# Gates gathered one step sooner, the last expert's table in the eighth step, expert results added as whole rows

## The chip, the cores and the metric

The kernel runs on one core of one Trainium2 chip. The metric is the device time of one execution in microseconds (us). A core has five engines with a queue each: TensorE (PE in the profile, its weight loads PEld), VectorE (DVE), ScalarE (ACT), GpSimd (POOL) and SyncE (SP), and 16 DMA engines that move data between the chip's memory (DRAM) and the core's own.

## The reference

One layer of a decoder on 512 new tokens and 64 tokens of running sequences, all in float32, width 1024. A mixer (a linear recurrence and a retention with running states) comes first. The part that matters here is the mixture of experts behind it: 16 experts in 4 groups, each token takes the best group and two experts in it.

```python
gates = jnp.sum(jax.nn.one_hot(expert_id, N_EXPERTS, dtype=F32)
                * (p_g[:, None] * top_w)[..., None], axis=1)
h = jax.nn.silu(jnp.einsum('nd,edf->nef', xf, w_g)) * jnp.einsum('nd,edf->nef', xf, w_u)
out = jnp.einsum('nef,efd->nd', h * gates[..., None], w_d)
```

Each expert has three matrices of 1 MB: `w_g` and `w_u` (1024 x 256) and `w_d` (256 x 1024). The result is normed, scaled and added to the tokens; the new retention states are outputs too.

## The kernel before

The first 350 us are the mixer and the routing; the change does not touch them. Then comes the loop over `NST` = 14 steps, numbered 0 to 13. Steps 0 to 2 hold experts 0 to 2, the others hold the remaining experts in the order of their token counts. Steps 5 and 9 (`paired(e)`) hold two small experts of up to 64 tokens each, all others one expert with up to 128. An expert's tokens are its up to 128 *slots*.

A step in the order in which it is worked on:

- `hits(e)` (VectorE, three steps ahead, `AHEAD` = 3) builds a 0/1 table of tokens by slots; `slot_tokens(e)` (TensorE, five small transposes or products) turns it into token numbers; `numbers(e)` (VectorE) writes them as indices.
- `gather_input(e)` (GpSimd, four indirect DMAs) fetches the tokens' rows to `xg`; `take_input(e)` (VectorE, one 128x1024 transpose, line 2443; for step 0 TensorE transposes and VectorE and ScalarE copy a half each, line 2435) turns them.
- `expert_in(e)` (TensorE) forms the gate and the up product, 32 instructions each; `pair_in(e)` does the same for a pair, in other PSUM banks. ScalarE takes silu of the first (semaphore `s_hs`), VectorE multiplies by the second (`s_hm`; line 2538, for a pair line 2534). A pair's product is transposed by `pair_turn`, in the middle of the next step's `expert_in`.
- `expert_out(e)`, `pair_out(e)` (TensorE) form the output, a pair's one step later. `take_out(e)` copies it times the gate to `eo[e % 2]`, ScalarE the first 512 columns (`s_eoa`), VectorE the last 512 (`s_eod`; lines 2453, 2457).
- The gates lie in `gates_dram`. `gather_gates(e)` (GpSimd, line 771) fetches the slots' rows of 16 gates to `gsl[e % 2]`; from step 3 on `pick_gates(e)` (VectorE, lines 2498 to 2502) picks the expert's column, and only then can `take_out(e)` run.
- `add_rows(e)` (GpSimd, line 782) adds `eo` to the tokens' rows in DRAM, with an indirect DMA that accumulates. There are two tables of 512 columns, `f_dram[0]` and `f_dram[1]`, and a chain of DMAs for each: each add waits (`s_ost`) until the add before it in its chain has landed, and `take_out(e)` waits until the add of step e - 2 has.

The last expert (step 13) is not added in DRAM: VectorE builds a table of tokens by slots times gate (`wlast`, lines 2543 to 2557, now in step 2), TensorE transposes it in steps 11 and 12 (`turn_last`) and multiplies it by the last results (`add_last`), while SyncE loads the sums from `f_dram` to `Y` (line 606). The closing chain on VectorE (`finish`) norms and adds.

All orders are written out by hand, one per engine. GpSimd's, in iteration j: `gather_input(j)`, `gather_gates(j - 2)`, `add_rows(j - 3)`. VectorE's, in step e: `hits(e + 3)`, the products, `take_input(e + 1)`, `numbers(e + 3)`, the pick, `take_out`. For step 9, a pair, `take_input(10)` comes ahead of the products. An engine works its list strictly in order. Before the loop VectorE has `numbers(2)`, `take_input(0)`, then `new_state` (heads 2 and 3 of the retention states, read from PSUM banks 4, 5, 1 and 6, line 2179; semaphore `s_snew`), then the gates (lines 2290 to 2521, `s_gw`). `expert_in(0)` waits for `s_snew` ahead of its up products, which write banks 1 and 6. The weights stream through 13 buffers of 1 MB, each loaded by SyncE as soon as TensorE is done with what it held.

Lines 811 and 814 are the helpers through which TensorE's products and transposes are recorded, line 1494 ScalarE's.

Of the kernel before, what the change touches and what calls it, by code (L numbers as in the profile page):

```python
# [16 lines left out]
P = 128  # L17
# [10 lines left out]
NH = 4  # L28
# [29 lines left out]
MORE = 4  # L58

# [122 lines left out]
def build(nc, x_prompt, x_sample, state_conv, state_lru, state_ret, c_prompt, c_sample, w_mod, b_mod,  # L182
# [6 lines left out]
    with ExitStack() as ctx:  # L189
# [3 lines left out]
        def sem(name):  # L193
# [8 lines left out]
        f_dram = [nc.dram_tensor(f"f_dram{c}", (6 * P, HALF), F32, kind="Internal").ap()  # L202
                  for c in range(2)]
# [97 lines left out]
        gsl = [region(14784 + i * NE, NE) for i in range(2)]  # L301
# [113 lines left out]
        s_ost = [[sem(f"s_ost{c}{i}") for i in range(2)] for c in range(2)]  # L415
# [79 lines left out]
        gpick = [tiny(144 + i, 1) for i in range(2)]  # L495
        lastr, lastg = tiny(152, TILES), tiny(160, TILES)
# [29 lines left out]
        def _(sp):  # L526
# [68 lines left out]
            with sp.Else():  # L595
# [4 lines left out]
                for t in END_ORDER:  # L600
                    for c in range(2):
                        if t == END_ORDER[0]:
                            sp.wait_ge(s_ost[c][0], 16 * (NST // 2))
                            sp.wait_ge(s_ost[c][1], 16 * ((NST - 1) // 2))
                        if t < TILES - 1:
                            sp.dma_start(Y[:, t, c * HALF:(c + 1) * HALF],
                                         f_dram[c][t * P:(t + 1) * P, :]).then_inc(s_fl[t], 16)
                        else:
                            sp.dma_start(Y[c * NS:(c + 1) * NS, t, 0:HALF], f_dram[c][SEQ:NTOK, :])\
# [19 lines left out]
        def _(pool):  # L629
# [54 lines left out]
            for c in range(2):  # L684
                pool.dma_start(f_dram[c].rearrange("(a p) d -> p a d", p=P),
                               consts[:, None, C_ZERO:C_ZERO + HALF].to_broadcast([P, 6, HALF]))\
                    .then_inc(s_fready, 16)
# [74 lines left out]
            with pool.Else():  # L762
                def gather_gates(e):
# [12 lines left out]
                def add_rows(e):  # L776
                    pool.wait_ge(s_add, e + 1)
                    for c in range(2):
                        pool.wait_ge((s_eoa, s_eod)[c], e + 1)
                        if e:  # L780
                            pool.wait_ge(s_ost[c][(e - 1) % 2], 16 * ((e - 1) // 2 + 1))
                        pool.indirect_dma_start(  # L782
                            out=f_dram[c], in_=eo[e % 2][:, c * HALF:(c + 1) * HALF],
                            in_offset=None, compute_op=ALU.add,
                            out_offset=bass.IndirectOffsetOnAxis(ap=add_tok[:, e:e + 1], axis=0),
                            bounds_check=NTOK - 1, oob_is_err=False)\
# [1829 lines left out]
```

## Time and profile before

| | before |
|---|---|
| median of 3 runs | 549.45 us (547.32 to 549.88) |
| the profiled execution | 548.57 us |
| its span | 546.6 us |
| mean granted clock of TensorE | 0.99 |
| TensorE busy | 522.1 us, 96% |
| VectorE busy | 259.3 us, 47% |
| GpSimd busy | 155.2 us, 28% |

The span is the time from the first to the last instruction in the trace; the rest of the profiled execution's time lies around it. All times in the trace count from the span's start. A line of a timeline gives start, length, engine, source line, operation, tiles (out<-in), shapes and how many instructions are merged in it; a bracket at its end is the idle time of the engine just before it and what ended that. The granted clock is 1.00 at 2.4 GHz and 0.50 at 1.2 GHz. "DMA to landing" is the time from an issue to the arrival of its last byte.

### The profile page before, as it was taken

What the parts mean: (1) busy time and instruction counts of PE and PEld (TensorE: products, weight loads), DVE (VectorE), ACT (ScalarE), POOL (GpSimd) and SP (SyncE); (2) the same over time, 40 slices, a digit from 0 to 9 for tenths busy, and PEclk for the clock granted to TensorE, in tenths of its full rate; (3) what the DMA queues carried; (4) which work ended last, traced back from release to release, by engine and by line L of the source; (5) the groups of instructions that cost most, each with busy time, mean ns of one, the idle gap of its engine ahead of it and who ended that gap; (6) DMA issues with size and microseconds to landing.
All of it is one profiled execution on the core that took longest, in us unless ns stands there. A gap on an engine that the chain in (4) does not pass through costs nothing.

```text
span 546.6 us, 7575 instructions
## 1 busy us (share of the span) xinstructions
PE 522.1 (96%) x2798; PEld 324.0 (59%) x2798; DVE 259.3 (47%) x759; ACT 151.3 (28%) x293; POOL 155.2 (28%) x166
## 2 busy tenths in 40 slices
PE   8999999999999999999999999788999899899994
PEld 6677755544455454557444445477787777577851
DVE  3443465443033143244453365684776545643347
ACT  7332497711123122132232333400010010000132
POOL 3017000116000000000210020347777747756500
PEclk8999999999999999999999999999999999999998
DMA  9999997899800000009820034879997999996474
GB/s 267 356 328 354 348 321 312 305 387 361 291 0 1 0 0 1 1 4 383 327 78 38 38 116 172 311 278 387 362 362 259 351 396 367 366 377 221 56 196 177
DMA packets 47417, 126.50 MB, mean 231 GB/s; under 512 B 6654, under 2 KB 19358, under 8 KB 41234
## 3 DMA queue, kind: packets, MB, share of 16 engines
q1 hardware_dynamic: 30912, 99.36, 49.6%
q0 software_dynamic: 11408, 22.05, 15.0%
q10 hardware_dynamic: 5058, 4.58, 2.5%
q8 instruction: 24, 0.39, 0.3%
q14 instruction: 15, 0.12, 0.1%
HBM read 116.48 MB, written 17.30 MB: 245 GB/s over the span
## 4 chain that ended last, share of the span: by engine, by line
PE 73%; DMA 10%; DVE 8%; issue 5%; POOL 3%; SPq 1%; ACT 0%; POOLq 0%; ACTq 0%; DVEq 0%
PE psum L811 71%; DMA arena<-gates_dram,slot_tok 5%; DMA ring<-in_w_mod_dram 3%; POOL arena L753 2%; PE psum L814 2%; DMA u_dram<-arena 2%; DVE arena L2378 1%; DVE x L2383 1%; DVE arena L2443 1%; DVE arena L2325 1%; DVE arena L2179 0%; SPq L574 0%; DVE arena L2457 0%; DVE arena L2319 0%; ACT arena L1494 0%
## 5 line engine op out<-in xcount | busy, mean ns | idle before, releaser
L811 PE MATMUL psum<-ring,uT 128*128 128x512 f32 (+1 forms) x384 | 126.5, 522 | 0.0
L811 PEld LDWEIGHTS psum<-ring,uT 128*128 128x128 f32 (+1 forms) x384 | 56.5, 172 | 60.1 <-issue 55.8
L1494 ACT ACTIVATE arena<-psum 128x512 f32<-128x512 f32 (+6 forms) x80 | 35.7, 476 | 164.7 <-PE psum L811 154.0
L811 PE MATMUL psum<-uT,ring 128*128 128x288 f32 x256 | 64.9, 410 | 0.1
L811 PEld LDWEIGHTS psum<-arena,ring 128*128 128x128 f32 x512 | 60.1, 196 | 6.8 <-issue 6.8
L811 PE MATMUL psum<-arena,ring 128*128 128x128 f32 x512 | 60.6, 280 | 3.7 <-DVE arena L2534 2.1
L753 POOL DMA_INDIRECT arena<-u_dram,part_tok x52 | 53.4, 1028 | 21.6 <-issue 14.3
L811 PEld LDWEIGHTS psum<-uT,ring 128*128 128x128 f32 x256 | 47.7, 190 | 16.4 <-issue 4.0
L811 PE MATMUL psum<-ring,arena 128*64 128x256 f32 (+2 forms) x192 | 50.6, 490 | 0.1
L782 POOL DMA_INDIRECT f_dram<-arena,add_tok x26 | 41.6, 1600 | 27.7 <-issue 13.1
L811 PE MATMUL psum<-arena 128*128 128x128 f32 (+6 forms) x253 | 42.3, 330 | 5.4 <-DVE arena L2325 2.4
L1494 ACT ACT_TABLE_LOAD x33 | 42.3, 1283 | 3.1 <-issue 2.1
L811 PEld LDWEIGHTS psum<-arena 128*128 128x128 f32 (+4 forms) x253 | 26.3, 157 | 21.0 <-issue 16.4
L811 PEld LDWEIGHTS psum<-ring,arena 128*64 128x64 f32 (+1 forms) x192 | 22.4, 154 | 22.8 <-issue 18.4
L699 POOL DMA_DIRECT2D out_dram<-arena x1 | 0.8, 829 | 123.8 <-DVE arena L2117 123.8
L811 PE MATMUL psum<-ring,hy 128*128 128x512 f32 (+1 forms) x80 | 32.9, 600 | 0.5 <-ACT arena L1494 0.5
L811 PE MATMUL psum<-ring,outbT 128*128 128x512 f32 (+1 forms) x80 | 32.4, 593 | 0.0
L1494 ACT ACTIVATE arena<-psum,uT 128x512 f32<-128x512 f32 x10 | 6.9, 688 | 77.2 <-DVE uT L2502 54.2
L2443 DVE STREAM_TRANSPOSE arena<-arena 128x1024 f32<-128x1024 f32 x13 | 26.4, 2028 | 0.0
L1494 ACT ACTIVATE arena<-psum,con 128x128 f32<-128x128 f32 x36 | 10.4, 368 | 53.1 <-PE psum L811 45.5
L2086 DVE TENSOR_TENSOR arena<-arena,con 128x512 f32<-128x512 f32 (+1 forms) x10 | 6.3, 634 | 36.6 <-ACT arena L1494 32.8
L814 PEld LDWEIGHTS psum<-con,arena 128*128 128x128 f32 (+1 forms) x147 | 18.0, 153 | 9.6 <-issue 6.5
(261 smaller groups left out, 603.9 us busy)
## 6 DMA issues: line engine op xcount, KB each, us to landing
ring<-in_w_mod_dram SPq DMA_DIRECT2D x24, 1024.0 KB, 11.9
ring<-in_w_exp_down_dram SPq DMA_DIRECT2D x12, 1024.0 KB, 13.5
ring<-in_w_exp_gate_dram SPq DMA_DIRECT2D x11, 1024.0 KB, 9.7
ring<-in_w_exp_up_dram SPq DMA_DIRECT2D x11, 1024.0 KB, 12.4
ring<-in_w_in_dram SPq DMA_DIRECT2D x10, 1024.0 KB, 10.4
ring<-in_w_out_dram SPq DMA_DIRECT2D x4, 1024.0 KB, 7.0
uT<-in_w_exp_gate_dram SPq DMA_DIRECT2D x4, 1024.0 KB, 13.1
f_dram<-in_consts_dram POOLq DMA_DIRECT2D x2, 1536.0 KB, 16.8
```

The source lines that it names most:

```text
L699: pool.dma_start(ret_prompt[0, 0].rearrange("h k e -> k h e"), S.rearrange("p (h e) -> p h e", e=DK)).then_inc(s_store, 16)
L753: pool.indirect_dma_start(out=xg[e % 2][:, b * QD:(b + 1) * QD], out_offset=None, in_=u2_dram.rearrange("n (g c) -> (n g) c", g=PARTS), in ...
L782: pool.indirect_dma_start(out=f_dram[c], in_=eo[e % 2][:, c * HALF:(c + 1) * HALF], in_offset=None, compute_op=ALU.add, out_offset=bass.In ...
L811: return nc.tensor.matmul(out, lhsT, rhs, start=first, stop=last)
L814: return nc.tensor.transpose(out, src, ident[0:src.shape[0], 0:src.shape[0]])
L1494: return nc.scalar.activation(out, src, func, **kw).then_inc(done, 1)
L2086: v.tensor_tensor(out=each(dst), in0=each(src), in1=cs, op=ALU.mult)
L2325: last = v.tensor_scalar(hit[e % 2][:, t, :], iota16[:], col, None, ALU.is_equal)
L2378: v.scalar_tensor_tensor(out=Y[:, t, o], in0=src[:, o], scalar=ss[:, 3, t, 0:1], in1=tab["g2" + tag(t)][:, o], op0=ALU.mult, op1=ALU.mult)\
L2383: v.tensor_tensor(out=x[:, t, o], in0=x[:, t, o], in1=Y[:, t, o], op=ALU.add)\
L2443: v.transpose(xgT[e % 2].rearrange("p k (b s) -> p k b s", s=BLK), xg[e % 2].rearrange("p (b q k) -> p k b q", b=PARTS, k=KT))\
```

## The change

Three parts and some order. First, `gather_gates(e)` is issued in GpSimd's iteration e + 1, no longer e + 2, into one of four buffers. It waits for the gather two steps before, and for the results of step e - 4. Second, `f_dram` is one table of 1024 columns, and `add_rows` is one DMA with one chain; its `eo` buffer is free when that has landed. Third, the last expert's table is built in step 7 (`LAST_AT`). Besides, `pair_in` and the `expert_in` behind a pair wait for less, while `pair_turn` waits for both products of the pair at once; and ahead of the loop VectorE copies step 0's input before `numbers(2)` and forms the gates before it updates the states.

```diff
@@ GpSimd: gather_gates, add_rows and the loop
                     if e >= 2:
-                        pool.wait_ge(s_eoa, e - 1)
-                        pool.wait_ge(s_eod, e - 1)
+                        pool.wait_ge(s_gs[e % 2], 16 * (e // 2))
+                    if e >= 4:
+                        pool.wait_ge(s_eoa, e - 3)
+                        pool.wait_ge(s_eod, e - 3)
                     pool.indirect_dma_start(
-                        out=gsl[e % 2], out_offset=None, in_=gates_dram,
+                        out=gsl[e % 4], out_offset=None, in_=gates_dram,
...
                 def add_rows(e):
                     pool.wait_ge(s_add, e + 1)
-                    for c in range(2):
-                        pool.wait_ge((s_eoa, s_eod)[c], e + 1)
-                        if e:
-                            pool.wait_ge(s_ost[c][(e - 1) % 2], 16 * ((e - 1) // 2 + 1))
-                        pool.indirect_dma_start(
-                            out=f_dram[c], in_=eo[e % 2][:, c * HALF:(c + 1) * HALF],
...
+                    pool.wait_ge(s_eoa, e + 1)
+                    pool.wait_ge(s_eod, e + 1)
+                    if e:
+                        pool.wait_ge(s_ost[(e - 1) % 2], 16 * ((e - 1) // 2 + 1))
+                    pool.indirect_dma_start(
+                        out=f_dram, in_=eo[e % 2], in_offset=None, compute_op=ALU.add,
...
-                    if 2 <= e < NST + 1:
-                        gather_gates(e - 2)
+                    if e == 2:
+                        gather_gates(0)
+                    if 2 <= e < NST:
+                        gather_gates(e - 1)
@@ TensorE: pair_in, pair_turn, expert_in
                     pe.wait_ge(s_xgTd, e + 2)
-                    pe.wait_ge(s_hs, e)
-                    pe.wait_ge(s_hm, FT * e)
+                    earlier = [i for i in range(e) if paired(i)]
+                    if earlier:
+                        pe.wait_ge(s_eoa, earlier[-1] + 1)
+                        pe.wait_ge(s_eod, earlier[-1] + 1)
...
                 def pair_turn(e):
+                    pe.wait_ge(s_hm, FT * (e + 1))
                     for k in range(FT):
-                        pe.wait_ge(s_hm, FT * e + k + 1)
...
                     if e >= 1:
-                        pe.wait_ge(s_hs, e)
-                        pe.wait_ge(s_hm, FT * e)
+                        done = e - paired(e - 1)
+                        pe.wait_ge(s_hs, done)
+                        pe.wait_ge(s_hm, FT * done)
@@ ScalarE and VectorE: take_out
-                        act.wait_ge(s_ost[0][e % 2], 16 * (e // 2))
+                        act.wait_ge(s_ost[e % 2], 16 * (e // 2))
...
-                        dve.wait_ge(s_ost[1][e % 2], 16 * (e // 2))
+                        dve.wait_ge(s_ost[e % 2], 16 * (e // 2))
@@ VectorE: ahead of the loop, and in it
                 orders()
+                take_input(0)
                 numbers(2)
-
-                take_input(0)
-                for h in range(2, NH):
-                    new_state(h)
                 gate_weights()
...
                 v.tensor_tensor(out=gates[:], in0=oh[0], in1=oh[1], op=ALU.add).then_inc(s_gw, 1)
+                for h in range(2, NH):
+                    new_state(h)
...
-                    if e == 2:
+                    if e == LAST_AT:
                         dve.wait_ge(s_gw, 2)
```

SyncE's loads of the sums wait for the one chain and read each half out of the wide table.

## Rows read from the trace of the kernel before

**Rows 1.** the page, part 1: busy us, share of span, instructions
```profile
PE 522.1 (96%) x2798; PEld 324.0 (59%) x2798; DVE 259.3 (47%) x759; ACT 151.3 (28%) x293; POOL 155.2 (28%) x166
```

**Rows 2.** TensorE's timeline, 359 to 482 us: start, length, what [idle before, releaser]
```profile
359.10 1.04 PE L814 MATMUL psum<-con,arena 128*128 128x128 f32 x8
361.66 7.38 PE L811 MATMUL psum<-arena,ring 128*128 128x128 f32 x64 [1.51 <-DVE arena L2435]
368.88 0.44 PE L811 MATMUL psum<-arena 128*128 128x128 f16 x5
369.16 3.65 PE L811 MATMUL psum<-ring,arena 128*128 128x512 f32 x8
372.65 7.31 PE L811 MATMUL psum<-arena,ring 128*128 128x128 f32 x64
381.47 0.79 PE L811 MATMUL psum<-arena 128*128 128x128 f16 x5 [1.51 <-DVE arena L2325]
382.31 3.67 PE L811 MATMUL psum<-ring,arena 128*128 128x512 f32 x8
...
426.87 3.81 PE L811 MATMUL psum<-arena,uT 128*128 128x128 f32 x32 [0.71 <-DVE arena L2534]
...
430.74 3.74 PE L811 MATMUL psum<-arena,uT 128*128 128x128 f32 x32
...
436.54 7.29 PE L811 MATMUL psum<-ring,arena 128*64 128x512 f32 x24
...
454.58 7.31 PE L811 MATMUL psum<-arena,ring 128*128 128x128 f32 x64
...
463.23 4.03 PE L811 MATMUL psum<-ring,arena 128*128 128x512 f32 x9
...
473.89 0.72 PE L811 MATMUL psum<-arena 128*128 128x128 f16 x5
476.75 5.44 PE L811 MATMUL psum<-arena,ring 128*128 128x128 f32 x32 [2.14 <-DVE arena L2534]
```

**Rows 3.** windows: us, busy PE, PEld, DVE, ACT, POOL, granted clock, DMA share, GB/s
```profile
382.30:425.70 43.40, 43.39 (x303) 32.89 (x303) 30.87 (x108) 3.90 (x7) 32.28 (x28) 1.00 0.94 327
...
476.75:482.20 5.45, 5.45 (x34) 5.45 (x35) 1.35 (x9) 0.00 (x0) 3.96 (x3) 0.69 1.02 393
```

**Rows 4.** waits view: total us, times, longest
```profile
DVE uT L2498 <- DMA arena<-gates_dram,slot_tok: 26.4, 7, 5.1
```

**Rows 5.** GpSimd's timeline: the gates' gather of step 8
```profile
463.80 0.97 POOL L771 DMA_INDIRECT arena<-gates_dram,slot_tok  x1 [0.30 <-issue]
```

**Rows 6.** VectorE's timeline: start, steps 0, 8 and 9, the tail
```profile
359.13 0.28 DVE L2333 TENSOR_TENSOR arena<-psum,con 128x128 f32<-128x128 f32 x1
...
360.83 0.69 DVE L2435 COPY arena<-psum 128x512 f32<-128x512 f32 x1
361.43 2.47 DVE L2179 SCALAR_TENSOR_TENSOR arena<-arena,psum 128x512 f32<-128x512 f32 x4
...
365.27 0.24 DVE L2521 TENSOR_TENSOR gates<-arena 128x80 f32<-128x80 f32 x1
...
379.68 0.75 DVE L2453 TENSOR_SCALAR arena<-psum,arena 128x512 f32<-128x512 f32 x1 [6.71 <-DMA arena<-gates_dram,slot_tok]
...
472.03 0.75 DVE L2457 TENSOR_SCALAR arena<-psum,uT 128x512 f32<-128x512 f32 x1
...
474.24 2.00 DVE L2443 STREAM_TRANSPOSE arena<-arena 128x1024 f32<-128x1024 f32 x1
...
529.76 1.22 DVE L2572 TENSOR_TENSOR arena<-psum,arena 128x1024 f32<-128x1024 f32 x1 [0.92 <-PE psum L811]
```

**Rows 7.** DMA issues, 450.9 to 451.3 us: us to landing
```profile
outbT<-in_w_exp_up_dram SPq DMA_DIRECT2D x1, 1024.0 KB, 16.5
```

**Rows 8.** tile f_dram, 381 to 470 us: the half-row adds
```profile
L782 POOL DMA_INDIRECT f_dram<-arena,add_tok x16: 1582/1607/1652, 381.3 to 468.6; - x16
...
DMA to landing us min/median/max: 8.1/9.5/11.6
```

More of the change, by code:

```diff
@@ L58 @@
 MORE = 4
+LAST_AT = 7
 LOG_G = [math.log1p(-(2.0 ** (-5.0 - h))) for h in range(NH)]
@@ L201, in build @@
         gates_dram = nc.dram_tensor("gates_dram", (NTOK, NE), F32, kind="Internal").ap()
-        f_dram = [nc.dram_tensor(f"f_dram{c}", (6 * P, HALF), F32, kind="Internal").ap()
-                  for c in range(2)]
+        f_dram = nc.dram_tensor("f_dram", (6 * P, D), F32, kind="Internal").ap()
         psum = ctx.enter_context(nc.psum_tensor("psum", [P, 8 * 512], F32))
@@ L300, in build @@
         rank1 = region(14336 + 3 * TILES * NE, TILES, NE)
-        gsl = [region(14784 + i * NE, NE) for i in range(2)]
         spare = region(14816, 1)
@@ L414, in build @@
         s_eod = sem("s_eod")
-        s_ost = [[sem(f"s_ost{c}{i}") for i in range(2)] for c in range(2)]
+        s_ost = [sem(f"s_ost{i}") for i in range(2)]
         s_add = sem("s_add")
@@ L495, in build @@
         gpick = [tiny(144 + i, 1) for i in range(2)]
+        gsl = [tiny(432 + i * NE, NE) for i in range(4)]
         lastr, lastg = tiny(152, TILES), tiny(160, TILES)
@@ L602, in _ @@
                         if t == END_ORDER[0]:
-                            sp.wait_ge(s_ost[c][0], 16 * (NST // 2))
-                            sp.wait_ge(s_ost[c][1], 16 * ((NST - 1) // 2))
+                            sp.wait_ge(s_ost[0], 16 * (NST // 2))
+                            sp.wait_ge(s_ost[1], 16 * ((NST - 1) // 2))
                         if t < TILES - 1:
                             sp.dma_start(Y[:, t, c * HALF:(c + 1) * HALF],
-                                         f_dram[c][t * P:(t + 1) * P, :]).then_inc(s_fl[t], 16)
-                        else:
-                            sp.dma_start(Y[c * NS:(c + 1) * NS, t, 0:HALF], f_dram[c][SEQ:NTOK, :])\
+                                         f_dram[t * P:(t + 1) * P, c * HALF:(c + 1) * HALF])\
+                                .then_inc(s_fl[t], 16)
+                        else:
+                            sp.dma_start(Y[c * NS:(c + 1) * NS, t, 0:HALF],
+                                         f_dram[SEQ:NTOK, c * HALF:(c + 1) * HALF])\
                                 .then_inc(s_fl[t], 16)
@@ L684, in _ @@
             for c in range(2):
-                pool.dma_start(f_dram[c].rearrange("(a p) d -> p a d", p=P),
+                pool.dma_start(f_dram[:, c * HALF:(c + 1) * HALF].rearrange("(a p) d -> p a d", p=P),
                                consts[:, None, C_ZERO:C_ZERO + HALF].to_broadcast([P, 6, HALF]))\
@@ L777, in add_rows @@
                     pool.wait_ge(s_add, e + 1)
-                    for c in range(2):
-                        pool.wait_ge((s_eoa, s_eod)[c], e + 1)
-                        if e:
-                            pool.wait_ge(s_ost[c][(e - 1) % 2], 16 * ((e - 1) // 2 + 1))
-                        pool.indirect_dma_start(
-                            out=f_dram[c], in_=eo[e % 2][:, c * HALF:(c + 1) * HALF],
-                            in_offset=None, compute_op=ALU.add,
-                            out_offset=bass.IndirectOffsetOnAxis(ap=add_tok[:, e:e + 1], axis=0),
-                            bounds_check=NTOK - 1, oob_is_err=False)\
-                            .then_inc(s_ost[c][e % 2], 16)
+                    pool.wait_ge(s_eoa, e + 1)
[4 more added lines that the diff above has]
+                        out=f_dram, in_=eo[e % 2], in_offset=None, compute_op=ALU.add,
+                        out_offset=bass.IndirectOffsetOnAxis(ap=add_tok[:, e:e + 1], axis=0),
+                        bounds_check=NTOK - 1, oob_is_err=False).then_inc(s_ost[e % 2], 16)
                 for e in range(NST + 2):
@@ L1840, in take_out @@
                         f(eo[e % 2][:, 0:512], bank[4], ACT.Copy, s_eoa,
-                          scale=gsl[e % 2][:, e:e + 1])
+                          scale=gsl[e % 4][:, e:e + 1])
                     elif e < NST - 1:
@@ L2499, in pick_gates @@
                                              float(at + 1), None, ALU.is_equal))
-                    link(v.tensor_tensor(out=masked[:, 0], in0=gsl[e % 2][:, FIRST:NE], in1=mine,
+                    link(v.tensor_tensor(out=masked[:, 0], in0=gsl[e % 4][:, FIRST:NE], in1=mine,
                                          op=ALU.mult))
```

2 lines of the change are left out of this document (1 added, 1 removed).

## The prediction, made before the changed kernel was run

> **What bounds the kernel now.** I read the page first: TensorE is busy 96% of the span [rows 1], so time can only come out of its waits, or out of whatever runs after its last product. TensorE's own timeline of the expert loop comes next, and the reader should look at the brackets and at the gaps between lines [rows 2]. From 382.31 to 426.16 us (426.87 less the wait in its bracket) it has no gap; the windows view has 43.39 of 43.40 us busy there [rows 3]. Elsewhere it waits, and each time for VectorE: 1.51 us before step 0, 1.51 us before the five small transposes `slot_tokens(4)`, 0.71 us before step 6, and later the gaps 434.48 to 436.54, 461.89 to 463.23 and 474.61 to 476.75. A normal passage from one matmul group over `slot_tokens` to the next takes about 0.3 us (368.88 to 369.16). After the longest wait its clock is lower: the granted clock of the next 5.45 us is 0.69 [rows 3], a mix of the 2.4 and the 1.2 GHz level, and 32 products take 5.44 us that take 3.74 elsewhere [rows 2]. What preceded the fall is that wait of 2.14 us right behind `slot_tokens`.
>
> The waits view says why VectorE is late: it waits 26.4 us in seven steps for the gates that GpSimd gathers [rows 4]. In step 8 GpSimd issues that gather at 463.80, after four input gathers [rows 5]; VectorE can pick gates and take the result out only at 472.03, and the order written by hand then makes `hits(12)`, `take_input(10)` and the products of step 9 late [rows 6]. So the first gates set the wait at 381.47, and the late gathers set those from 434 to 476 us.
>
> **The start, where a wait is added.** Today VectorE runs `numbers(2)` from 359.13, copies its half of the input at 360.83, then updates the states (361.43 to 363.90) and forms the gates until 365.51 [rows 6]. Changed, the copy (0.69) can begin when TensorE's eight transposes are done, at 360.14 (359.10 + 1.04 [rows 2]); with a little for the semaphore, TensorE starts step 0 at 361.0 instead of 361.66. Then follow `numbers(2)` (1.70) to 362.6, the gates (1.61) to 364.2, and only then the states (2.47) to 366.7. TensorE's first half of step 0, 32 products, takes 3.6 us, to 364.6. Its second half waits for the states, `s_snew`, because it writes the banks they are read from. That is a new wait of 2.1 us, and step 0 ends at 370.4 instead of 369.0, plus 1.4. Behind this wait on TensorE stands all that follows; nothing covers it.
>
> In exchange the gates are ready 1.3 us sooner. GpSimd's queue behind them is unchanged (two writes, four gathers, `gather_gates(0)`), so `take_out(0)` moves from 379.68 to 378.4 [rows 6], and the gather for step 1 now follows it. `hits(4)` behind it takes at most 1.9 us (the transposes that follow it end at 382.26, and it can begin only behind `take_out(0)`, 380.43 today), so it is done by 381.1. Step 1 of TensorE ends at 370.4 + 0.3 + 3.5 (369.16 to 372.65) + 7.3 = 381.5 [rows 2]. Its wait of 1.51 is gone, with 0.4 us to spare, and the next products start at 381.8 instead of 382.31: minus 0.5 for start and wait together.
>
> **The gates a step sooner.** `gather_gates(e)` is issued one step before the pick, so VectorE's 26.4 us vanish and its work moves up. Where a pair came before, `expert_in` no longer waits for the pair's products, only `pair_turn` does, 3.7 us later. Step by step against rows 2: before step 6, minus 0.71; before the pair's output, 2.06 becomes 0.3, minus 1.76; before step 8's output, 1.34 becomes 0.3, minus 1.04; before step 10, 2.86 (473.89 to 476.75) becomes 0.4, minus 2.46; and without that wait the clock does not fall, 5.44 becomes 3.74, minus 1.70. The sum is 0.50 + 0.71 + 1.76 + 1.04 + 2.46 + 1.70 = 8.2 us.
>
> The added waits on `s_gs` and on results three steps back are for things long done. The last expert's table, eight small operations, moves from step 2 to step 7. By the sum above TensorE then runs 2.97 us earlier, so step 7 begins at about 440.7 and its products are there at 448.2. After them VectorE has a transpose (2.0 us [rows 6]), `numbers` (1.7), the table (2.6, an estimate from such small operations), the pick (0.5), `take_out` (0.75) and `hits(11)` (1.9): done at 457.7, and TensorE asks at 461.89 - 2.97 = 458.9. It costs nothing with 1.2 us of cover; without cover it would cost up to 2.6.
>
> **Weights.** A faster TensorE needs them sooner. The tightest that I find is the up matrix of step 10: issued at 451.0, landed 16.5 us later, 467.5 [rows 7]. Step 10 will begin at 473.89 - 4.01 + 0.3 = 470.2 and want this matrix 3.6 us later, at 473.8. Cost nothing, with 6 us of cover even if no transfer comes sooner.
>
> **Whole rows in one chain.** 26 adds of 1.6 us become 13 [rows 8]. The trace has no 1024-wide add. For GpSimd I bound one instruction by 1.6 (rows counted) and 3.2 us (bytes counted); it has slack either way, and the queue gets 0 to 20 us shorter, which TensorE does not see. The landing matters, since each add waits for the one before. One half lands in 9.5 us (median; 8.1 to 11.6) [rows 8]. Two halves, the second issued 1.9 us later (1.6 + 0.3 of issue [rows 5, 8]), are down 1.9 + 9.5 = 11.4 us after the first issue, at worst 13.5. These are my two ends: 9.5 for a whole row, if the number of rows counts, and 11.4, at worst 13.5, if bytes do. I take 10.5, since there are as many rows as in one half and the second half's setup goes.
>
> When does it cost? The first add goes out at 381.3 [rows 8]. Seven landings later, `take_out(8)` may use its buffer; to keep TensorE fed at 470.2, VectorE must begin it by 470.2 - 0.5 - 2.0 - 1.9 - 0.75 = 465.0. With 0.3 us between landing and issue, the chain holds up to (465.0 - 381.3) / 7 - 0.3 = 11.7 us a landing; each further microsecond costs 7. At 9.5, 10.5 or 11.4 the cost is nothing.
>
> Of the landing, the rows show that q0 takes 9.5 us in this stretch while weights stream. The Trainium skill (DMA: Bandwidth & Descriptors, section Queues, rings and completion order) says that each DMA engine goes round its queues a packet at a time; wider rows would then wait for fewer turns. By that rule the landing would be nearer 9.5, by bytes nearer 11.4, and the sum is 8.2 in both.
>
> **The tail.** The adds' last landing and the loads of `f_dram` come a little sooner, but from 529.76 VectorE runs its closing chain, and that line waits for TensorE [rows 6]. So the tail moves as a block and yields nothing of its own.
>
> **The rivals.** (A) The new wait of 2.1 us in step 0 lowers the clock as the one at 474.61 did. For it: the length is the same. Against it: full work stands just before it, whereas the other had `slot_tokens` only. Price 1.7, time 542.1. (B) The chain of whole rows holds the buffers: landings near 12.2 cost 7 x 0.5 = 3.5 us, with a fall of the clock 5.2, time 545.6. (C) The other side: landings of 13.5 us on average, the worst of the two halves. Then `take_out(8)` is 7 x 1.8 = 12.6 us late, and with the clock 14.3: 6.1 us slower than now, 554.7. It decides from 12.6 us a landing on, where the gain of 8.2 is used up. Against it, 13.5 is built from a maximum, not a median. (D) The change doesn't do what it says: VectorE stays late for another reason, such as inputs gathered too late (`take_input` waits instead). GpSimd's queue gets shorter, which speaks against; the time would be 547 to 549.
>
> **How the numbers follow.** The profiled execution took 548.57 us, span 546.6 and 2.0 around it. Minus 8.2 that is 540.4. It lies 0.9 below the median shown, 549.45, whose own shift would give 541.3; I say 540.8. Chances: forecast 0.66, A 0.13, B 0.08, C 0.04, D 0.09. The range goes from 538.3 (the start costs nothing after all, minus 9.7, and a run as fast as the fastest) to 546 (B and the cheap side of D). A change of 0.5%, 2.7 us, is about what measurements of this kernel can tell from none. Faster beyond it: the forecast, A and B, 0.87, with a little of D 0.88. Same: most of D, 0.07. Slower: C and a remainder, 0.05.
>
> **What the next profile would show.** Right: VectorE no longer waits for gates; TensorE has a wait of about 2 us after its first 32 products, for the states' update, and then no gap over 0.5 us to its end; no low clock near 470. Wrong: TensorE or VectorE waiting for `f_dram` adds, adds landing over 12 us after their issue, or a granted clock under 1 behind step 0. The prediction fails most easily through the chain of adds, whose landing no row shows.

## The result and the profile after

| | before | changed |
|---|---|---|
| median in one comparison, 5 runs each | 548.41 us (547.32 to 549.88) | 543.45 us (541.91 to 544.01) |
| ratio | | 0.9897 (95%: 0.9868 to 0.9926) |
| the profiled execution, its span | 548.57, 546.6 | 543.37, 541.6 |
| mean granted clock | 0.990 | 0.994 |

The changed kernel is 1.0% faster: 5.0 us by the medians, 5.0 by the two spans. I had forecast 540.8 us, in a range from 538.3 to 546, a gain of 8.2 by the trace. So 3 us are missing, and the profile shows where.

The page's first part, and the line of its costliest groups for the adds (busy us, mean ns, then idle before and releaser):

```profile
PE 518.8 (96%) x2798; PEld 321.9 (59%) x2798; DVE 258.4 (48%) x759; ACT 151.3 (28%) x293; POOL 133.7 (25%) x153
...
L786 POOL DMA_INDIRECT f_dram<-arena,add_tok x13 | 20.9, 1608 | 36.6 <-DMA f_dram<-arena,add_tok 18.4
```

13 adds take 1608 ns each, as the 26 half rows did [rows 8], so GpSimd loses 21.5 us of work [rows 1]. In return it now sits 18.4 us before adds, waiting for the add before to land.

TensorE's timeline of the changed kernel, the places of [rows 2] and the end:

```profile
358.79 1.04 PE L818 MATMUL psum<-con,arena 128*128 128x128 f32 x8
360.70 3.81 PE L815 MATMUL psum<-arena,ring 128*128 128x128 f32 x32 [0.88 <-DVE arena L2442]
366.31 3.84 PE L815 MATMUL psum<-arena,ring 128*128 128x128 f32 x32 [1.80 <-DVE arena L2186]
...
381.81 3.67 PE L815 MATMUL psum<-ring,arena 128*128 128x512 f32 x8
...
425.50 3.79 PE L815 MATMUL psum<-arena,uT 128*128 128x128 f32 x32
...
433.29 7.28 PE L815 MATMUL psum<-ring,arena 128*64 128x512 f32 x24
...
458.75 4.01 PE L815 MATMUL psum<-ring,arena 128*128 128x512 f32 x9
...
469.39 0.45 PE L815 MATMUL psum<-arena 128*128 128x128 f16 x5
470.43 3.81 PE L815 MATMUL psum<-arena,ring 128*128 128x128 f32 x32 [0.59 <-issue]
...
518.02 3.71 PE L815 MATMUL psum<-arena 128*128 128x512 f32 x8
523.04 2.13 PE L815 MATMUL psum<-arena 128*64 128x512 f32 x6 [1.31 <-DVE arena L2585]
527.03 1.13 PE L815 MATMUL psum<-arena,con 128*128 128x512 f32 x2 [1.86 <-DMA arena<-f_dram]
```

The reader is to see that the first lines are the forecast ones, almost to the tenth: the copy lets step 0 start at 360.70 (I said 361.0), the new wait for the states is 1.80 us (2.1), the second half starts at 366.31 (366.7), step 1's output at 381.81 (381.8). From there to 518.02 only one bracket is left. The line at 518.02 is `add_last`, the first product behind step 13; in the kernel before the same line stood at 526.02:

```profile
526.02 5.77 PE L811 MATMUL psum<-arena 128*128 128x512 f32 x14
```

There all 14 products ran without a pause. Now only 8 do, and then TensorE waits twice, once directly for `f_dram`. Call what lies from this line's start to the span's end the tail: 546.6 - 526.02 = 20.6 us before, 541.6 - 518.02 = 23.6 after. TensorE gained 8.0 us, and the tail gave 3.0 back.

The chain that ended last says why. Changed kernel, 482 to 530 us (start, length, what):

```profile
482.43 0.76 DVE arena L2464
...
484.13 9.22 DMA f_dram<-arena,add_tok
...
494.24 9.44 DMA f_dram<-arena,add_tok
...
504.55 6.91 DMA f_dram<-arena,add_tok
...
512.30 5.98 DMA f_dram<-arena,add_tok
518.34 0.34 SPq L606
...
519.67 5.00 DMA arena<-f_dram
...
524.77 0.06 DVE arena L2578
```

This is a queue of adds. Step 9 is a pair, so its result is taken out a step late, in 482.43 to 483.2; step 10's follows at 485.57, step 11's at 496.58, step 12's at 507.56:

```profile
481.94 0.69 ACT L1501 ACTIVATE arena<-psum,uT 128x512 f32<-128x512 f32 x1 [7.01 <-PE psum L815]
485.57 0.69 ACT L1501 ACTIVATE arena<-psum,uT 128x512 f32<-128x512 f32 x1 [2.93 <-PE psum L815]
496.58 0.69 ACT L1501 ACTIVATE arena<-psum,uT 128x512 f32<-128x512 f32 x1 [7.06 <-PE psum L815]
507.56 0.69 ACT L1501 ACTIVATE arena<-psum,uT 128x512 f32<-128x512 f32 x1 [7.02 <-PE psum L815]
```

Two results 3.6 us apart meet a chain that takes 10 us a link. Step 10's add goes out at 494.24, 8 us after its result, step 11's at 504.55, 7 us after, step 12's at 512.30, still 4 us after. The last landing is at 518.3, the first load of the sums into `Y` at 518.34 and not before, and VectorE's closing chain starts behind them at 524.77. In the kernel before the chain through the same stretch was TensorE's alone, up to VectorE's line at 529.76 [rows 6]:

```profile
511.89 17.85 PE psum L811 x88
529.76 0.04 DVE arena L2572
```

The first theory, formed from this: the single chain of whole rows finishes too late for the sums, and two chains of halves would give 3 us back. The rival theories: the missing part sits in TensorE's loop (the new wait in step 0, the 0.75 us before step 10), or late adds are due to the rows' width rather than to their queue.

### The profile page after: what moved, and what is told of

Read it like the earlier page. It is cut to its first block, busy times and chain, and to the rows that moved or that the text cites. A ratio compares the mean times of both kernels' runs of the same rounds, so it can differ in the third digit from the quotient of the medians.

```text
span 541.6 us, 7557 instructions
## 1 busy us (share of the span) xinstructions
PE 518.8 (96%) x2798; PEld 321.9 (59%) x2798; DVE 258.4 (48%) x759; ACT 151.3 (28%) x293; POOL 133.7 (25%) x153
## 4 chain that ended last, share of the span: by engine, by line
PE 80%; DMA 9%; DVE 6%; issue 2%; ACT 1%; SPq 0%; ACTq 0%; POOLq 0%; DVEq 0%
PE psum L815 77%; DMA f_dram<-arena,add_tok 6%; PE psum L818 3%; DMA u_dram<-arena 2%; DVE arena L2385 1%; DMA arena<-f_dram 1%; DVE x L2390 1%; DMA hy<-in_c_sample_dram 1%; DVE arena L2186 0%; ACT arena L1501 0%; DVE arena L2450 0%; ACT L1501 0%; DVE arena L1922 0%; DVE arena L2332 0%; SPq L606 0%
## 5 line engine op out<-in xcount | busy, mean ns | idle before, releaser
L815 PEld LDWEIGHTS psum<-arena,ring 128*128 128x128 f32 x512 | 58.5, 192 | 6.6 <-issue 4.6
L815 PE MATMUL psum<-arena,ring 128*128 128x128 f32 x512 | 59.2, 275 | 3.3 <-DVE arena L2186 1.8
L815 PE MATMUL psum<-arena 128*128 128x128 f32 (+6 forms) x253 | 41.1, 329 | 3.9 <-issue 1.9
L1501 ACT ACTIVATE arena<-psum,uT 128x512 f32<-128x512 f32 x13 | 8.9, 687 | 91.4 <-PE psum L815 46.3
L786 POOL DMA_INDIRECT f_dram<-arena,add_tok x13 | 20.9, 1608 | 36.6 <-DMA f_dram<-arena,add_tok 18.4
L2544 DVE TENSOR_TENSOR arena<-arena,psum 128x128 f32<-128x128 f32 x24 | 6.8, 286 | 42.0 <-PE psum L815 42.0
## 6 DMA issues: line engine op xcount, KB each, us to landing
ring<-in_w_in_dram SPq DMA_DIRECT2D x10, 1024.0 KB, 10.1
```

The source lines that it names most:

```text
L786: pool.indirect_dma_start(out=f_dram, in_=eo[e % 2], in_offset=None, compute_op=ALU.add, out_offset=bass.IndirectOffsetOnAxis(ap=add_tok[: ...
L815: return nc.tensor.matmul(out, lhsT, rhs, start=first, stop=last)
L1501: return nc.scalar.activation(out, src, func, **kw).then_inc(done, 1)
L2544: v.tensor_tensor(out=hT[e % 2][:, o], in0=hb[e % 2][:, o], in1=bank[(1, 6)[m]][:, 0:P], op=ALU.mult)\
```

## The experiments

The profile's columns that matter are the same in every run, so they stand in one table, which gives times from each run's own trace: the start of step 0's products, how long from there to `add_last` ("loop"), and from there to the span's end ("tail"). The start of step 0 differs by some microseconds between runs for reasons in the first 350 us, which the change does not touch; loop and tail are free of that. Neither counts what VectorE's new order gains ahead of step 0: from the start of the eight transposes to that of step 0 it is 1.91 us in the changed kernel (358.79 to 360.70) and 2.56 us before.

| kernel | median us (n) | ratio to before, 95% | step 0 starts | loop | tail |
|---|---|---|---|---|---|
| before | 548.41 (5) | 1 | 361.66 | 164.4 | 20.6 |
| changed | 543.45 (5) | 0.9897 (0.9868 to 0.9926) | 360.70 | 157.3 | 23.6 |
| changed, measured again | 544.12 (4) | 0.9900 (0.9857 to 0.9942) | 361.43 | 157.4 | 23.5 |
| two chains of halves | 540.34 (6) | 0.9828 (0.9801 to 0.9855) | 363.48 | 156.5 | 20.6 |
| before + whole rows | 550.11 (10) | 1.0005 (0.9981 to 1.0029) | 362.00 | 162.2 | 24.9 |
| before + gates sooner | 543.26 (4) | 0.9893 (0.9859 to 0.9927) | 361.84 | 157.6 | 20.6 |
| states ahead of gates | 545.37 (10) | 0.9919 (0.9894 to 0.9943) | 360.63 | 158.7 | 24.4 |
| adds of steps 10, 11 left out | 539.90 (4) | 0.9832 (0.9811 to 0.9852) | 361.60 | 156.6 | 20.9 |
| old waits of TensorE | 545.23 (4) | 0.9922 (0.9894 to 0.9950) | 367.37 | 157.7 | 24.0 |
| table in step 2 | 543.85 (5) | 0.9918 (0.9879 to 0.9957) | 361.71 | 157.0 | 23.3 |
| halves, states split, `hits(4)` first | 540.11 (5) | 0.9836 (0.9812 to 0.9860) | 362.48 | 155.3 | 21.3 |
| halves with old waits | 542.55 (4) | 0.9876 (0.9838 to 0.9913) | 361.87 | 158.4 | 20.7 |
| up matrix waited for later | 542.72 (1) | | 360.23 | 156.5 | 24.2 |

The experiments were measured in three comparisons, each with the kernel before beside it, whose median was 549.69, 548.71 and 548.88 us; the ratios go by that.

**Two chains of halves.** The changed kernel, but the table, the adds and their semaphores as before:

```diff
-                    pool.wait_ge(s_eoa, e + 1)
-                    pool.wait_ge(s_eod, e + 1)
...
-                        out=f_dram, in_=eo[e % 2], in_offset=None, compute_op=ALU.add,
...
+                    for c in range(2):
+                        pool.wait_ge((s_eoa, s_eod)[c], e + 1)
...
+                            out=f_dram[c], in_=eo[e % 2][:, c * HALF:(c + 1) * HALF],
```

> The changed kernel with two tables of 512 columns and two chains of adds again, nothing else undone. Theory 1 (the single chain of whole rows is late at the end): the last add then lands before TensorE's last product again, the closing chain waits for TensorE and not for f_dram, and the 3.0 us that the tail grew come back: span 538.6 us against 541.6, ratio to the kernel before 0.984 to 0.986. Theory 2 (the tail is late because the faster loop puts the last adds beside the last weights, whatever their width): the last add still lands after TensorE's last product, and the gain is under 1 us, span 540.6 to 541.6.

Ratio 0.9828, some 3 us below the changed kernel, though its profiled run began step 0 2.8 us later. The chain that ended last is TensorE's again up to VectorE's closing line:

```profile
505.81 17.85 PE psum L816 x88
523.69 0.04 DVE arena L2579
```

The tail is 20.6 us, the same as before. The first theory's size is right: whole rows in one chain cost 3.1 us between the medians, and of the change as made they are a loss. By the ratios, and by loop plus tail of the two traces (177.1 against 180.9), the difference is 3.8 us: 3.0 of it is the tail, the rest lies in the loop, where TensorE did not wait before step 10 in this trace.

**Whole rows alone.** The kernel before with that part only.

```diff
-        f_dram = [nc.dram_tensor(f"f_dram{c}", (6 * P, HALF), F32, kind="Internal").ap()
-                  for c in range(2)]
+        f_dram = nc.dram_tensor("f_dram", (6 * P, D), F32, kind="Internal").ap()
```

> The kernel before with the one table and the one chain of whole-row adds, nothing else changed. Theory 1: the loads for the closing chain had only 0.2 us to spare before (landed 529.5, wanted 529.76), and the last whole-row add lands about 1 us later than the second half did: the time rises by 0.5 to 1.5 us, ratio 1.001 to 1.003, and VectorE waits for f_dram at the start of the closing chain. Theory 2: no difference, within 0.3 us. If instead the chain of adds were a burden in the loop too, the ratio would be 1.005 or more and VectorE's take_out would wait for adds.

Nothing that can be measured: 1.0005 (0.9981 to 1.0029), an interval that holds both theories. Its one trace shows two things that pull against each other. TensorE's timeline, the waits of the loop and the tail:

```profile
461.66 0.79 PE L810 MATMUL psum<-arena 128*128 128x128 f16 x5 [1.31 <-DVE arena L2324]
462.50 5.73 PE L810 MATMUL psum<-ring,arena 128*128 128x512 f32 x9
...
476.06 3.81 PE L810 MATMUL psum<-arena,ring 128*128 128x128 f32 x32 [0.74 <-DVE arena L2533]
...
529.71 2.87 PE L810 MATMUL psum<-arena 128*64 128x512 f32 x6 [1.83 <-DVE arena L2578]
533.42 2.07 PE L810 MATMUL psum<-arena,con 128*128 128x512 f32 x2 [0.83 <-DMA arena<-f_dram]
```

The wait of 2.14 us before step 10 and the slow products behind it [rows 2] are gone, but a wait of 1.31 us and slow products now stand before step 8's output: nine of them take 5.73 us instead of 4.03 [rows 2], at a granted clock of 0.71 between 462.50 and 468.30. In sum the loop is 2.2 us shorter. The gates come a little sooner: step 8's gather goes out 101.4 us after step 0's start instead of 102.1. I had written that TensorE doesn't see GpSimd's shorter queue. This trace speaks against that, since the gates' gather stands behind the adds in that queue, but it is one trace beside one, and the medians don't show it. The tail is 4.3 us longer: VectorE's closing line waits for the loads of the sums, as the first theory had it, and the products behind TensorE's wait took 2.87 us instead of 2.13, so the clock fell as well (0.72 between 529.7 and 532.6).

**Gates sooner alone.** The kernel before with `gather_gates` in iteration e + 1 and four buffers.

```diff
-                    if 2 <= e < NST + 1:
-                        gather_gates(e - 2)
+                    if e == 2:
+                        gather_gates(0)
+                    if 2 <= e < NST:
+                        gather_gates(e - 1)
```

> The kernel before with the gates gathered one step sooner into four buffers, nothing else changed. If the late gates were what stalled steps 6 to 10, then 1.8 + 1.0 + 1.9 us of waits and the 1.7 us of low clock go, the pair's products (0.6 us each before steps 6 and 10) and the 1.5 us before the transposes of step 1 stay, and the tail, with two chains, costs nothing: span 540.2 us, ratio about 0.988, as good as or better than the whole change. Rival: the reordered waits of pair_in and expert_in carry a good part of the gain; then a wait of 2 us before step 10 stays and the span is over 542.5.

```profile
381.38 0.79 PE L815 MATMUL psum<-arena 128*128 128x128 f16 x5 [1.25 <-DVE arena L2329]
...
426.79 3.81 PE L815 MATMUL psum<-arena,uT 128*128 128x128 f32 x32 [0.71 <-DVE arena L2538]
...
471.86 3.81 PE L815 MATMUL psum<-arena,ring 128*128 128x128 f32 x32 [0.71 <-DVE arena L2538]
```

The start's waits stay (1.52 us before step 0, 1.25 before `slot_tokens(4)`), the gaps from 434 to 476 fall to 0.71 us (the pair's products, for which this kernel still waits), and the tail doesn't grow. The span, 540.0 us, is the expected one, and the rival, a wait of 2 us before step 10, is out. This one edit gives the whole measured gain, 0.9893 against 0.9897.

**States ahead of gates.** The changed kernel with VectorE's old order of these two: step 0's new wait goes, the gates come later.

```diff
                 numbers(2)
+                for h in range(2, NH):
+                    new_state(h)
                 gate_weights()
...
-                for h in range(2, NH):
-                    new_state(h)
                 for e in range(NST):
```

> The changed kernel with the states of heads 2 and 3 updated ahead of the gates again, as before. Theory: TensorE's wait of 1.8 us in step 0 goes, but the gates come 2.4 us later, and so do take_out(0) and hits(4): TensorE waits about 2.5 to 3 us before the transposes of step 1 instead, net 0 to 1 us slower than the changed kernel, span 541.6 to 542.6. Rival: the reordering at the start is a pure loss, since another wait than that for the gates ends last in step 1; then it is 1 to 1.8 us faster than the changed kernel.

```profile
364.62 3.84 PE L815 MATMUL psum<-arena,ring 128*128 128x128 f32 x32 [0.18 <-DVE arena L2186]
...
381.20 0.90 PE L815 MATMUL psum<-arena 128*128 128x128 f16 x5 [1.82 <-DVE arena L2332]
382.04 5.12 PE L815 MATMUL psum<-ring,arena 128*128 128x512 f32 x8
```

The wait of 1.80 us in step 0 shrinks to 0.18, and 1.82 us come back before `slot_tokens(4)`. Behind that wait eight products take 5.12 us instead of 3.67. The windows view (us, busy PE, granted clock, DMA share, GB/s) has them between the levels of 2.4 and 1.2 GHz, at 0.71:

```profile
381.90:387.20 5.30, 5.30 (x12) 0.71 1.03 421
```

Loop plus tail is 183.1 us against 180.9. Of these 2.2 us, 1.4 lie in the loop, as much as the slow products cost (5.12 - 3.67). The others lie in the tail, where in this trace the clock fell too (0.54 between 528.5 and 532.0), which nothing ties to the order. The wait before `slot_tokens(4)` was shorter than the expected 2.5 to 3 us; the price of the clock was not in the expectation. The intervals overlap (0.9894 to 0.9943 against 0.9868 to 0.9926), so that forming the gates first gains 1.4 us is the reading of two traces, and the medians point the same way.

**Two adds left out.**

```diff
                 def add_rows(e):
+                    if e in (10, 11):
+                        return
```

> The changed kernel (whole rows, one chain) without the adds of steps 10 and 11, so that their results are missing from the output. Theory (the last add is late because it stands behind the chain, not because it is wide): the add of step 12 is issued as soon as its results are there, about 4 us sooner, lands in the same 6 us before TensorE's last product, and the tail is back at 20.6 us: span 538.6 us, as with two chains. Rival (the width of the last add and of the loads is what counts): the tail shortens by less than 1 us, span over 540.6.

This tells queue from width: the rows stay 1024 wide, only the backlog goes. The chain that ended last:

```profile
507.72 0.76 DVE arena L2467
...
509.42 6.09 DMA f_dram<-arena,add_tok
...
515.57 0.34 SPq L606
```

Step 12's add now goes out at once, 0.9 us behind its result, the loads start at 515.57, and TensorE runs its 14 products from 518.18 without a pause. The time is 539.9 us (0.9832), as with two chains. So nearly all of the 3 us is backlog. A small rest is not: the tail is 20.9 us and not 20.6, since the last landing, though 2.7 us ahead of `add_last`, still lets VectorE's closing line start 0.4 us later than TensorE would.

**TensorE's waits.** The changed kernel with the old waits behind a pair (`expert_in`, `pair_in`, `pair_turn`), in both forms of the adds:

```diff
-                        done = e - paired(e - 1)
-                        pe.wait_ge(s_hs, done)
-                        pe.wait_ge(s_hm, FT * done)
+                        pe.wait_ge(s_hs, e)
+                        pe.wait_ge(s_hm, FT * e)
```

> The changed kernel with the waits of pair_in, pair_turn and expert_in as before. Theory: TensorE waits 0.7 us for the pair's products before steps 6 and 10 each, and, since the tail stands on the chain of adds, only a part of these 1.4 us reaches the end: span 542.0 to 543.0. Rival: the wait before step 10 is 2 us with a fall of the clock, as in the kernel before; then 544 to 545.5.

> The changed kernel with two chains of half rows and with the waits of pair_in, pair_turn and expert_in as before. With two chains the end follows TensorE, so the two waits of 0.7 us should now be seen in full: 1.4 us over the 540.3 of two chains alone, 541.2 to 542.2. Rival: they vanish, because VectorE or the weights are what TensorE would wait for next; then 540.0 to 540.8.

With whole rows: 545.23 us, runs from 543.65 to 550.84, and 0.9922 (0.9894 to 0.9950) overlaps the changed kernel's 0.9897; that leaves it open. Its trace, of the slowest of the four, has both waits at 0.71 us and the full clock behind them, so the rival is out. With halves: 542.55 against 540.34 us. In its trace the two waits are back:

```profile
427.57 3.81 PE L816 MATMUL psum<-arena,uT 128*128 128x128 f32 x32 [0.71 <-DVE arena L2538]
...
472.64 3.81 PE L816 MATMUL psum<-arena,ring 128*128 128x128 f32 x32 [0.71 <-DVE arena L2538]
```

Each puts the next products 1.16 us behind the start of `slot_tokens` (426.41 to 427.57, 471.48 to 472.64) instead of 0.29, so together 1.74 us; the loop is 1.9 us longer. The intervals of the two ratios overlap a little (0.9838 to 0.9913, 0.9801 to 0.9855); that the loops of the two traces differ by what the two waits add is the better evidence. The relaxed waits are worth under 2 us, where the tail follows TensorE.

**The last table in step 2.** `LAST_AT` = 2 instead of 7.

> The changed kernel with the last expert's table built in step 2 again. Theory: VectorE has time there as well, 0 us: span 541.6, TensorE without a wait in steps 2 and 3. Rival: the 2.6 us of VectorE make hits(5) or take_input(4) late, plus 0.5 to 2 us.

543.85 us, and no wait on TensorE in steps 2 and 3. Loop plus tail is 180.3 against 180.9 us. Moving the table gains and costs nothing. One of the five runs, 1379.65 us, is far outside all others and not explained; the median isn't moved by it.

**Halves, states split, `hits(4)` first.** Two chains again; besides, VectorE updates head 3 first, whose banks the up products write, step 0's second half waits for it alone, and `hits(4)` comes ahead of `take_out(0)`.

```diff
-                            pe.wait_ge(s_snew, 4)
+                            pe.wait_ge(s_snew, 2)
...
-                for h in range(2, NH):
-                    new_state(h)
+                new_state(3)
+                new_state(2)
```

> The changed kernel with two chains of half rows, with head 3's states (whose banks step 0's up product takes) updated before head 2's and TensorE waiting for those alone, and with hits(4) ahead of take_out(0). Theory: TensorE's wait in step 0 shrinks from 1.8 to 0.6 us, and the wait for the gates no longer holds up the transposes of step 1: 1.2 to 1.6 us less than with two chains alone, so about 539 us, ratio to the kernel before 0.980. Rival: the first gates land at 379.2 us whatever TensorE does, and its second output waits for take_out(0) until 380; then the gain is 0.5 to 1 us only.

```profile
366.90 3.84 PE L816 MATMUL psum<-arena,ring 128*128 128x128 f32 x32 [0.61 <-DVE arena L2189]
```

The wait falls from 1.80 to 0.61 us and the loop to 155.3, the shortest of all. The time doesn't follow: 540.11 against 540.34 us. The chain that ended last holds adds again, now of half rows:

```profile
512.02 4.70 DMA f_dram<-arena,add_tok
```

So here the chain of halves is the bound: the loop is 1.2 us shorter than with two chains alone, as expected, and the tail takes 0.7 of it back (21.3 us against 20.6). The half microsecond that is left is too small for the medians.

**The up matrix waited for later.** `expert_in` waits for both its matrices at its head. Here it waits for the up matrix just ahead of the up products.

```diff
-                    wu = weights(pe, ("wu", e, 0)).rearrange("p (k n) -> p k n", n=FE)
...
+                        if w is wu:
+                            weights(pe, ("wu", e, 0))
```

> The changed kernel in which TensorE waits for an expert's up matrix only ahead of the up product. Theory (step 10 starts 0.75 us late because its up matrix, wanted at the head of expert_in, lands at 470.35): the gap behind the transposes of step 9 is 0.3 us again, as behind step 5. Rival (take_input(10) or the gate matrix is late): the gap of 1 us stays. The time itself should not move, since the end stands on the chain of adds.

```profile
468.87 0.45 PE L815 MATMUL psum<-arena 128*128 128x128 f16 x5
469.15 3.79 PE L815 MATMUL psum<-arena,ring 128*128 128x128 f32 x32
```

The gap goes from 1.04 to 0.28 us. But this run can't tell the theory from its rival, because the matrix came sooner in it: issued at 447.2 and landed 21.3 us later, at 468.5, it was there before `slot_tokens` began at 468.87, and the old wait would have cost nothing either. What speaks for the theory is when step 10's products start in the traces that have the gap: 0.09 us behind the landing of this matrix in each, at 470.43 behind 470.34 in the changed kernel, 471.25 behind 471.16 when it was measured again, 471.71 behind 471.62 with the states ahead of the gates, 471.12 behind 471.03 with the table in step 2.

The loop goes from 157.3 to 156.5; the tail takes back 0.6 of 0.8. That is what a bound elsewhere looks like: the last landing is 518.3 - 360.7 = 157.6 us after step 0's start in the changed kernel and 517.3 - 360.2 = 157.1 here.

**The changed kernel again.**

> The changed kernel once more, beside the next two, as the mark for them: ratio to the kernel before 0.987 to 0.993.

544.12 us, 0.9900 (0.9857 to 0.9942), the same as the first time. Its trace has the place before step 10 worse:

```profile
471.25 3.81 PE L815 MATMUL psum<-arena,ring 128*128 128x128 f32 x32 [1.34 <-issue]
```

That is 1.79 us behind `slot_tokens` at 469.46, against 1.04 in the first trace and 0.29 in that of the two adds left out. How late this matrix is varies from run to run.

## Why the prediction was right in direction and too large in size

The sum of 8.2 us, step by step; the last two columns are how much earlier than before the named line starts, and what each place adds to that:

| place | forecast | measured, so far | this place |
|---|---|---|---|
| start and `slot_tokens(4)`, to 381.81 | -0.50 | -0.50 | -0.50 |
| step 6, at 425.50 | -0.71 | -1.37 | -0.87 |
| the pair's output, at 433.29 | -1.76 | -3.25 | -1.88 |
| step 8's output, at 458.75 | -1.04 | -4.48 | -1.23 |
| step 10, at 470.43 | -2.46 | -6.32 | -1.84 |
| the clock behind it, `add_last` at 518.02 | -1.70 | -8.00 | -1.68 |
| the tail | 0 | -5.0 | +3.0 |

**The loop** came out as argued: 8.0 of 8.2 us. The first row is right partly by luck. The eight transposes ahead of step 0 began 0.31 us sooner in this run than before, which is not the change's doing. And `take_out(0)` moved only to 379.16, not to 378.4, so that `hits(4)` was done at 381.47, not by 381.1, and the small transposes behind it took 0.84 us instead of 0.3. VectorE waits for gathered gates only once more, 5.1 us in step 0, where they can't come sooner. The forecast granted clock holds too: from 425.20 to 518.00 us the windows view has 1.00 throughout, and TensorE busy 92.21 of 92.80.

```profile
425.20:518.00 92.80, 92.21 (x641) 70.11 (x640) 48.69 (x173) 10.10 (x21) 44.53 (x39) 1.00 0.90 312
```

**The weights** were the one miss in the loop. I called the up matrix of step 10 free, with 6 us of cover. Two things were wrong: it is needed at the head of the step, not 3.6 us in, since `expert_in` waits for both; and its landing took 22.6 us, not 16.5 [rows 7]:

```profile
outbT<-in_w_exp_up_dram SPq DMA_DIRECT2D x1, 1024.0 KB, 22.6
```

Issued at 447.75, it was there at 470.34, 0.09 us ahead of step 10's first product. Price 0.75 us in the first trace.

**The failing step is the tail.** I wrote that it "moves as a block and yields nothing of its own". I looked at the one line that waits for TensorE and did not ask by how much the adds' landing had missed being that line. In the kernel before the last half row goes out at 518.92 and lands 5.2 us later, at 524.1, 1.9 us ahead of `add_last`, as the trace of before has it:

```profile
518.92 1.56 POOL L782 DMA_INDIRECT f_dram<-arena,add_tok  x1 [0.30 <-issue]
```

The margin at the end was smaller than these 1.9 us, because the landing is followed by the loads of the sums. VectorE's closing line needs TensorE, 3.7 us behind the start of `add_last` (526.02 to 529.76), and the first four loads. In the kernel before the fourth load goes out at 525.00 and lands 4.5 us later, at 529.5, 0.3 us ahead of that line, and the line of VectorE before it did wait for a load:

```profile
arena<-f_dram SPq DMA_DIRECT2D x1, 256.0 KB, 4.5
...
527.56 0.69 DVE L2579 TENSOR_TENSOR arena<-psum,arena 128x512 f32<-128x512 f32 x1 [0.73 <-DMA arena<-f_dram]
```

In the changed kernel the fourth load goes out at 519.67 and lands at 524.67, and the closing line starts at 524.77; TensorE alone would have let it start at 518.02 + 3.74 = 521.76. That is the 3.0 us of the tail. They add up: the last landing moved from 1.9 us ahead of `add_last` to 0.3 behind it, 2.2 us; from the last landing to that of the fourth load it takes 6.4 us instead of 5.3, since with one chain no load can go out before the last landing (518.34), while the first one went out 1.4 us ahead of it before (522.70); less the margin of 0.3. In all thirteen traces the closing line starts 3.7 to 3.8 us behind the start of `add_last` or 0.1 us behind the fourth load's landing, whichever is later.

A block moved 8 us earlier needs the adds 8 us earlier, and the chain can't do that. The working that was missing could be done from the trace of before: step 9's first add goes out at 491.47 there, 8.2 us less is 483.3, and the four landings of steps 9 to 12 in a row at 9.5 to 10.5 us each give 521.3 to 525.3, behind an `add_last` that I had at 517.8. It came to 518.3, since the last two landed in 6.9 and 6.0 us once traffic thinned (DMA share 0.36 from 504 to 518 us, 0.87 in the 20 us before). I had tested the chain only where it could hold back `take_out(8)`, seven links in, and it was right there: nobody waits for a buffer. The consumer at its end was not tested. The experiments carry this: two chains give the tail its 20.6 us back, two adds fewer bring it to 20.9.

**The landing** of a whole row was taken as 10.5 us. The view of the tile `f_dram` in the changed kernel has, for the eight adds in the stretch of [rows 8], 381 to 470 us:

```profile
DMA to landing us min/median/max: 8.1/10.1/11.7
```

With 10.1 it is nearer the 9.5 of a half [rows 8] than the 11.4 that bytes would give. The Trainium skill (DMA: Bandwidth & Descriptors, section Queues, rings and completion order) has each DMA engine go round its queues a packet at a time. That wide rows wait for fewer turns was my conclusion from it: the trace leans that way, with 10.1, and shows nothing of the turns themselves. So the single link was well sized. What two chains have over one shows at the end: with little traffic the last half row landed in 4.4 us and the last whole row in 6.0, and the first loads can go out behind the first of the two chains.

**The rivals.** A, a fall of the clock behind step 0's wait: no, the 32 products behind it take 3.84 us at a granted clock of 1.00. B and C, buffers held in the middle of the loop: no, landings were 11.7 us at most, and the tile's view names no engine but GpSimd that waits for an add. D: no. B had the right object and the wrong victim.

**What the parts are worth**, from the runs: gates sooner some 6 us by themselves (549.69 to 543.26); relaxed waits under 2; VectorE's order ahead of the loop about 2, by the traces (1.4 from the gates ahead of the states, 0.65 from the copy ahead of `numbers(2)`); the table nothing; whole rows -3 in this company, nothing alone. The best measured versions that add all results are the change without its whole rows, 540.3 us, and the same with the states split and `hits(4)` first, 540.1; the two can't be told apart. That this is about where I had put the whole change is chance: the forecast had the whole rows in it, at no cost.

What stays open: why the time between the issue of a weight matrix and its landing varies so much between runs, and whether a chain of halves that starts sooner would let the shorter loop of the split states show.

## What to carry to other kernels

When a stretch gets faster, ask of everything that runs beside it and meets it at the end by how many microseconds it was early at the line that uses it. Here that was 0.3 us at VectorE's closing line against a gain of 8, and the trace of before gave a sign of it, a wait of 0.73 us for a load of the sums just ahead of that line. A serial chain of DMAs has to be followed link by link to its last consumer, from the place where results come closest together, and not only to the one buffer it might hold. Halving the number of DMAs in such a chain can cost more than it saves: here two chains of half rows side by side beat one of whole rows by 3 us.

## What the runs showed of the hardware beyond that

- An indirect add of rows twice as wide takes GpSimd the same time, 1.61 us, and lands 0.6 us later in the median while weights stream (10.1 against 9.5 us, 381 to 470 us); with less traffic beside it, the last two landed in 6.9 and 6.0 us, against 4.4 for the last half row in the run with two chains.
- A wait of 1.80 us between two full groups of 32 products left the granted clock at 1.00; one of 1.82 us ahead of five small transposes was followed by 0.71. One of 1.51 in that same place left the next eight products at their full rate [rows 2], and one of only 1.31 us ahead of the five transposes before step 8's output, in the run with whole rows alone, was followed by 0.71 again. The price of each fall, by the slow products behind it, was 1.45 to 1.70 us. So the length of the wait alone doesn't decide it, and these runs don't show what does.
- The same weight matrix, the up matrix of step 10, landed 16.5 us after its issue in the kernel before and 19.1 to 23.3 us after it in the twelve other traces. Where it was late, it put the products up to 1.79 us behind the start of `slot_tokens`.
